# Layer norm mean in the convolution phase: GpSimd adds the channel blocks, TensorE multiplies once with ones

## What is computed

```python
def layernorm(x, g, b):
    xf = x.astype(jnp.float32)
    xc = xf - jnp.mean(xf, axis=-1, keepdims=True)
    var = jnp.mean(xc * xc, axis=-1, keepdims=True)
    y = xc * lax.rsqrt(var + EPS) * g.astype(jnp.float32) + b.astype(jnp.float32)
    return y.astype(x.dtype)

def conv_branch(glu_hist, w_dw, b_dw, conv_ln_g, conv_ln_b, w_conv_out, b_conv_out):
    y = lax.conv_general_dilated(glu_hist, w_dw[:, None, :], window_strides=(1,), padding='VALID',
                                 dimension_numbers=('NWC', 'WIO', 'NWC'),
                                 feature_group_count=D_CONV) + b_dw
    y = jax.nn.silu(layernorm(y, conv_ln_g, conv_ln_b))
    return y @ w_conv_out + b_conv_out
```

## Time and profile before

| what | us |
|---|---|
| median of 3 runs (lowest to highest) | 1423.94 (1419.48 to 1424.90) |
| the profiled execution, its own time | 1421.46 |
| its span, first to last instruction | 1419.9 |
| TensorE busy over the span | 1277.9 (90%) |
| VectorE busy over the span | 1095.1 (77%) |
| ScalarE busy | 709.5 (50%) |
| GpSimd busy | 272.9 (19%) |

### The profile page before, as it was taken

One profiled execution on the slowest core, in us unless ns is written; L12 is line 12 of the kernel. 1 busy time (PEld: TensorE's weight loads), 2 busy tenths in 40 slices (PEclk: granted clock), 3 DMA queues, 4 the chain that ended last, 5 costly groups with the idle time before them and its releaser, 6 DMA issues. The chain is left out here.

```text
span 1419.9 us, 23929 instructions
## 1 busy us (share of the span) xinstructions
PE 1277.9 (90%) x8761; PEld 769.3 (54%) x8761; DVE 1095.1 (77%) x1305; ACT 709.5 (50%) x1167; POOL 272.9 (19%) x276
## 2 busy tenths in 40 slices
PE   4899999967999999999999999989938999788875
PEld 2456666655666666666666666645524555344432
DVE  5778888875769999999995876536475999777783
ACT  4656656654244423442333654424115888666672
POOL 1282000000000000000000000000332677324322
PEclk9999999987799999999999999999968999999998
DMA  8500000022112212222121045374865999899962
GB/s 305 163 9 2 0 0 0 0 112 72 38 46 84 83 43 71 82 67 83 31 94 61 31 156 204 118 282 164 296 227 199 362 320 368 322 328 320 329 226 34
DMA packets 51051, 203.51 MB, mean 143 GB/s; under 512 B 14464, under 2 KB 15552, under 8 KB 38400
## 3 DMA queue, kind: packets, MB, share of 16 engines
q1 hardware_dynamic: 32032, 156.92, 30.3%
q0 software_dynamic: 16656, 36.84, 9.9%
q10 hardware_dynamic: 2304, 8.95, 1.6%
HBM read 180.92 MB, written 39.72 MB: 155 GB/s over the span
## 5 line engine op out<-in xcount | busy, mean ns | idle before, releaser
L1262 DVE SCALAR_TENSOR_TENSOR big<-c_region,c_taps,big 128x1024 f32 (+1 forms) x120 | 153.8, 1282 | 4.0 <-ACT caT L962 4.0
L72 PE MATMUL c_psb<-xnT,w_taken 128*128 128x364 f16 x456 | 146.3, 321 | 2.4 <-DVE f_w_l L1157 2.4
L73 PE MATMUL c_psb<-xnT,w_taken 128*128 128x364 f16 x456 | 146.2, 321 | 0.0
L74 PE MATMUL c_psb<-xnT,f_w_l 128*128 128x364 f16 x456 | 146.0, 320 | 0.0
L1262 DVE SCALAR_TENSOR_TENSOR caT<-c_region,c_taps,caT 128x1024 f32<-128x1024 f32 x112 | 143.5, 1282 | 0.0
L72 PE MATMUL o_psH<-e_gu,big 128*128 128x512 f16 x256 | 99.4, 388 | 1.6 <-issue 1.5
L73 PE MATMUL o_psH<-e_gu,big 128*128 128x512 f16 x256 | 99.2, 387 | 0.0
L74 PE MATMUL o_psH<-e_gu,big 128*128 128x512 f16 x256 | 99.1, 387 | 0.0
L72 PE MATMUL c_psa<-xnT,w_taken 128*128 128x364 f16 x312 | 99.1, 318 | 0.0
L74 PE MATMUL c_psa<-xnT,f_w_l 128*128 128x364 f16 x312 | 99.0, 317 | 0.0
L73 PE MATMUL c_psa<-xnT,w_taken 128*128 128x364 f16 x312 | 99.0, 317 | 0.0
(11 more groups left out here) (362 smaller groups left out, 3503.7 us busy)
## 6 DMA issues: line engine op xcount, KB each, us to landing
e_gu<-w_gu SPq DMA_DIRECT2D x34, 1024.0 KB, 27.0
w_taken<-w_feat SPq DMA_DIRECT2D x48, 512.0 KB, 3.7
e_d<-w_dn SPq DMA_DIRECT2D x17, 1024.0 KB, 25.9
xnT<-w_gu SPq DMA_DIRECT2D x14, 1024.0 KB, 32.8
big<-w_gu SPq DMA_DIRECT2D x14, 1024.0 KB, 33.8
c_region<-gates POOLq DMA_DIRECT2D x8, 1092.0 KB, 5.9
xnT<-w_dn SPq DMA_DIRECT2D x7, 1024.0 KB, 30.7
big<-w_dn SPq DMA_DIRECT2D x7, 1024.0 KB, 30.1
```

The costliest lines, as they stand in the source:

```text
L72: pe.matmul(out, stat[0], mov[0], start=start, stop=False)
L73: pe.matmul(out, stat[0], mov[1], start=False, stop=False)
L74: return pe.matmul(out, stat[1], mov[0], start=False, stop=stop)
L1262: dve.scalar_tensor_tensor(y_j, glu[:, p, j:j + SEQ], tap, y_j, op0=ALU.mult, op1=ALU.add).then_inc(tap_done, 1)
```

## The change

GpSimd gets a second task in the loop. It holds `y_sum`, a row of 128 x 1092 float32 in a part of `caT` that is free then. After the history of blocks 0 and 1 it copies `y[:, 0]` into it, and in each later turn k, from 2 to 7, it adds `y[:, k - 1]` behind the history's DMAs. TensorE no longer multiplies in the loop; at its end `mean` multiplies `y_sum` (blocks 0 to 6) and `y[:, 7]` with ones, two matmuls each for the prompt columns and one each for the last 68. The loop of GpSimd is written as two turns of its own and a loop over the other six. In the history the waits stand in another order; the new order waits for the same things.

```diff
+        y_sum = room32[:, SEQ + TAPS * TS:SEQ + TAPS * TS + TM]
+        sum_done = sem("c_sum")
...
+            def add_up(k):
+                pool.wait_ge(tap_done, NTAP * k)
+                pool.wait_ge(sum_done, 1 * (k - 1))
+                pool.tensor_tensor(y_sum, y_sum, row(y, k - 1), ALU.add).then_inc(sum_done, 1)
+
+            history(0)
+            history(1)
+            pool.wait_ge(tap_done, NTAP)
+            pool.tensor_copy(y_sum, row(y, 0)).then_inc(sum_done, 1)
+            with pool.Fori(2, KC) as k:
+                history(k)
+                add_up(k)
...
-            def mean(k, first=False, last=False):
-
-                pe.wait_ge(tap_done, NTAP * k + NTAP)
+            def mean():
+                pe.wait_ge(sum_done, 1 * (KC - 1))
+                pe.wait_ge(tap_done, NTAP * KC)
                 for n in range(2):
-                    done = pe.matmul(psm[:, n], ones[:], row(y, k)[:, n * 512:(n + 1) * 512], start=first, stop=last)
-                return done
+                    cols = slice(n * 512, (n + 1) * 512)
+                    pe.matmul(psm[:, n], ones[:], y_sum[:, cols], start=True, stop=False)
+                    pe.matmul(psm[:, n], ones[:], y[:, KC - 1, cols], start=False, stop=True)
+                pe.matmul(psb[:, 0, 0:TM - SEQ], ones[:], y_sum[:, SEQ:TM], start=True, stop=False)
+                pe.matmul(psb[:, 0, 0:TM - SEQ], ones[:], y[:, KC - 1, SEQ:TM], start=False, stop=True).then_inc(mean_mm, 1)
...
-                if p or not first:
-                    mean(k - 1, first)
...
-            mean(KC - 1, False, True)
-            for k in range(KC):
-                last = pe.matmul(psb[:, 0, 0:TM - SEQ], ones[:], y[:, k, SEQ:TM], start=k == 0, stop=k == KC - 1)
-            last.then_inc(mean_mm, 1)
+            mean()
```

More of the change, by code:

```diff
@@ L910, in _, with history @@
             pool.wait_ge(setup, 1)
-            with pool.Fori(0, KC) as k:
-                pool.wait_ge(hist_ld, 16 * k)
+            def history(k):
+                p = ds(k % 2, 1)
+                if not isinstance(k, int) or k:
+                    pool.wait_ge(hist_ld, 16 * k)
+                    pool.wait_ge(hist_st, 16 * k)
+                    pool.wait_ge(hist_ps, 16 * k)
                 pool.wait_ge(glu_free, k + 1)
-                pool.wait_ge(hist_st, 16 * k)
-                pool.wait_ge(hist_ps, 16 * k)
-                pool.dma_start(glu[:, ds(k % 2, 1), HIST + SEQ:].rearrange("p a (b n) -> p (a b) n", b=NSEQ)[:, :, 0:HIST],
+                pool.dma_start(glu[:, p, HIST + SEQ:].rearrange("p a (b n) -> p (a b) n", b=NSEQ)[:, :, 0:HIST],
                                A["stateT"][ds(k * P, P)]).then_inc(hist_ld, 16)
@@ L919, in _ @@
                 pool.dma_start(A["sc_prompt"][ds(k * P, P), :],
-                               glu[:, ds(k % 2, 1), SEQ:SEQ + HIST].rearrange("p a n -> p (a n)")).then_inc(hist_ps, 16)
+                               glu[:, p, SEQ:SEQ + HIST].rearrange("p a n -> p (a n)")).then_inc(hist_ps, 16)
                 pool.dma_start(A["sc_sample"][ds(k * P, P)],
-                               glu[:, ds(k % 2, 1), HIST + SEQ:].rearrange("p a (b n) -> p (a b) n", b=NSEQ)
+                               glu[:, p, HIST + SEQ:].rearrange("p a (b n) -> p (a b) n", b=NSEQ)
                                [:, :, DSEQ:]).then_inc(hist_st, 16)
+            def add_up(k):
[9 more added lines that the diff above has]
+                add_up(k)
             pool.wait_ge(hist_st, 16 * KC)
```

## The result

The changed kernel takes 1432.17 us (median of four runs, 1431.75 to 1432.53) against 1424.19 (the three runs of the kernel before and a fourth), a ratio of 1.0066 with a 95% interval of 1.0051 to 1.0082. Run again later beside other runs of the kernel before, it gave 1.0073 (1.0058 to 1.0088). The forecast was 1434.

A forecast was written before the change was run, and what follows sets the result against it. TensorE bounds the loop, VectorE 1 to 2 us behind per block. Copy 0.7, additions 11.4, waits -4.9, mean 0.5 and clock 2.3 make 10.0 us on 1423.9, so 1434, range 1419 to 1440.

The forecast's parts named there:

- The bound moves to VectorE, and the 12 us are worth only its waits: Convolution loop: TensorE loses 12.0 us of matmuls, but VectorE moves forward only by 4.9 us of waits (2.5 to 6.1).
- A streaming addition holds the tap: Blocks 2 to 7: GpSimd's 2.4 us addition delays VectorE's first tap by 1.9 us, 11.4 us in all.
- The copy in block 1: Block 1: GpSimd's copy takes 1.1 us and costs VectorE 0.7 us, between 0.3 and 1.2.
- End of the taps: End of block 7 on VectorE: 0.7 + 11.4 - 4.9 = 7.2 us later.
- Mean and clock: Mean after the loop: 0.5 us more matmul work, and some 2.3 us for a half-rate clock after TensorE idles.
- Sum: Whole kernel: 7.2 + 0.5 + 2.3 = 10.0 us slower.
- Side by side: Rival at the taps: both engines read together when GpSimd comes first, VectorE only moves forward; 1421.8 us, chance 0.18.
- turns column by column: Rival at the taps: engines alternate reads, each addition costs the taps 1.2 us; 1429.4 us, chance 0.15.
- starving: Rival: GpSimd never gets between taps, adds only during the block-end reduction, next state load late; 1430.8 us, chance 0.05.
- twice as long: Rival: the addition takes 4.8 us beside VectorE and the tap loses 4.3; 1448 us, chance 0.04.
- the full gain: Rival in the loop: TensorE's 12.0 us count in full; 1412 us, chance 0.03.
- The signs named: Profile after: first taps about 3.2 us, no VectorE wait for a, TensorE idle before the mean, line 1440 waiting for VectorE.

The follow-up runs named there:

- the run with both kinds of work: Kernel before, with GpSimd's copy and additions added, their sum unused, and TensorE's matmuls kept in the loop: 1434.54 us, ratio to before 1.0072.
- four columns: Changed kernel, but GpSimd adds only 4 of the 1092 columns in each block: 1423.73 us, ratio to before 1.0001.
- the kernel with the additions in the reduction: Changed kernel with GpSimd's copy and additions moved beside VectorE's one-input reduction at each block's end, next state load ahead: 1426.53 us, ratio to before 1.0021.
- the warmed kernel: Changed kernel with 24 extra matmuls, their result overwritten, between product 33 and the mean: 1431.67 us, ratio to before 1.0072.
- the run with additions in mid taps: Changed kernel with each GpSimd addition waiting for six taps of its block: 1437.00 us, ratio to before 1.0097.
- the kernel with the early sum: Changed kernel with TensorE's three matmuls on y_sum put ahead of the wait for block 7: 1429.31 us, ratio to before 1.0050.

## Why the prediction was right, and where its sizes were off

The forecast was 1434, the measured median 1432.2, and the mechanism is the forecast one. Step by step:

- *The bound moves to VectorE, and the 12 us are worth only its waits.* Right; the run with both kinds of work shows it directly. The term was mis-sized: I took 4.9 us of waits as avoidable, with a handover of 0.2 us, and 2.7 were. The handover is 0.40 us from even to odd blocks and 0.50 to 0.90 where the loop turns, 3.4 us in six. The prediction's upper bound of 0.6, from the smallest wait of 0.62, was good for the mean of 0.57 but not for each block, and the waits of blocks 4 and 6 had no room at all. The 2.7 us are near the lower bound of 2.5.
- *A streaming addition holds the tap.* Right, with 1.73 us against 1.9 forecast, 10.4 against 11.4 in all; its length was 2.58 us against 2.4. That length was met with luck: four columns take 0.29 us, so the fixed part is about half of the 0.57 taken from the earlier trace rows, and a column costs (2.58 - 0.29) / 1088 = 2.1 ns against 1.68. The two errors went against each other at 1092 columns. For the copy the memset's rate was right (1.09 us in the kernel with the additions in the reduction, 1.1 forecast). In the prediction's sentence on the 4497 ns, "half" is 1092 of 2048 columns. It started 0.7 us before the tap was issued, with no pause behind the store, instead of 0.5.
- *The copy in block 1.* 0.7 forecast. It lasted 1.22 us and held the second `low` of the block, which took 2.87 us, 1.65 longer than usual. VectorE had been idle for 0.47 us ahead of the first tap, which hid that much, and the tap came 1.1 us later in the chain (5.20 us behind the block's first instruction, 4.10 before).
- *End of the taps.* 7.2 us later forecast, 8.6 measured: 10.4 + 1.1 - 2.7 = 8.8, and 0.2 that I can't place.
- *Mean and clock.* 0.5 + 2.3 = 2.8 forecast, 2.1 measured from the taps' end to the first subtraction. The work itself was right (4.0 us at the full clock; 3.9 in the warmed kernel). The granted clock fell only some 5 us into the idle stretch, about when the mean began, and not after 2.9 as in the earlier trace rows, and it came back 3.6 us after the mean's start instead of 4.7. The part that ran slowly cost 1.65 us.
- *Sum.* 10.0 forecast, 10.7 in the traces; by the ratios 9.4 in the first comparison and 10.4 in the second, by the bare medians 8.0 and 9.4. That the sum came so close is in part luck: the waits gave 2.2 us less than forecast and the copy cost 0.4 more, while the additions cost 1.0 and the mean 0.7 less.
- *The rivals.* Side by side is refuted for these additions by each tap of 3 us; turns column by column by the tap's 1.09 us behind the addition's end; starving by the run with additions in mid taps; twice as long by 2.58 us; the full gain by the run with both. The signs named were right but for one: TensorE's wait ahead of the mean stands at line 1439, since both waits are queued ahead of the first matmul. Its position is what the kernel with the early sum changes. And the prediction's "no row shows one that comes first" overlooks its own, where the power came first.

## What to carry to other kernels

When two engines are nearly equally loaded, work taken from the busier one is worth only what the other one waits in vain; count those waits, and take off the handover that remains. GpSimd's additions and copies were not free beside VectorE here: for as long as they ran, VectorE's instructions with two SBUF inputs stood still, so put them beside instructions with one SBUF input, and make them no longer than those. Before a wait that ends on another engine, put whatever doesn't need that engine.

## What the hardware showed that I had not expected

- A waiting VectorE instruction doesn't get its turn between two GpSimd instructions that follow each other: it was held for both, 4.95 us.
- The copy held a `low` that the profile shows as started 0.56 us before it (431.35 against 431.91 us), and that ended 1.1 us behind the copy's end, as if it had not begun to read. In the run with additions in mid taps the tap that ran first was finished first. What made the difference stays open: no run tells whether GpSimd's store DMA just ahead of the copy had a part in it.
- Not every GpSimd instruction that reads holds a VectorE instruction with two SBUF inputs for its whole length: in the middle of the power of the earlier trace rows one kept its 0.16 us. That the power had read its 20 columns by then is the prediction's guess, and no run here tests it.
- The granted clock did not fall from 1.00 to 0.50 after a fixed idle time: some 2.9 us into a wait at 64 us, some 5 us into the one ahead of the mean, and in the kernel with the early sum about 2 us after its last matmul.
